# The end of the mixing in a two-block hybrid network on one core: y of the second token tile read first, x's row sums in one pass

## The reference

```python
h = rms_norm(x, g1)                 # first:  x * rsqrt(mean(x*x) + 1e-6) * g
mix = mixers(h @ w_in)              # four kinds of heads, 1024 columns
x = x + rms_norm(mix @ w_out, g2)   # y = mix @ w_out is normed by its own row sums
h = rms_norm(x, g3)
# first kind:  y = (gelu(dwconv(h @ w_gate)) * (h @ w_up)) @ w_down
# second kind: y = square(relu(h @ w_up)) @ w_down
x = x + rms_norm(y, g4)
# second kind also: x = x + sigmoid(x @ w_ple_gate) * (p @ w_ple_proj)
```

## Time and profile before

| | us |
|---|---|
| runs | 1693.14, 1697.64, 1698.69 (median 1697.64) |
| the profiled execution | 1691.87, its span 1689.8 |
| PE busy | 1594.9 (94%), granted clock 0.973 of full in the mean |
| DVE busy | 1093.3 (65%) |
| ACT busy | 776.6 (46%) |
| chain that ended last | PE 81%, DVE 10%, ACT 3% |

### The profile page before, as it was taken

One profiled execution on the slowest core, in us unless ns is written; L12 is line 12 of the kernel. 1 busy time (PEld: TensorE's weight loads), 2 busy tenths in 40 slices (PEclk: granted clock), 3 DMA queues, 4 the chain that ended last, 5 costly groups with the idle time before them and its releaser, 6 DMA issues.

```text
span 1689.8 us, 29634 instructions
## 1 busy us (share of the span) xinstructions
PE 1594.9 (94%) x12124; PEld 1425.8 (84%) x12124; DVE 1093.3 (65%) x1609; ACT 776.6 (46%) x1199; POOL 0.2 (0%) x4
## 2 busy tenths in 40 slices
PE   7998988999999989799999989999999979999998
PEld 7987568998898856799989877899889977799887
DVE  3866666776476665577754898666453798666545
ACT  4534254444435332544444455755344346655434
POOL 0000000000000000000000000000000000000000
PEclk9999898999999989899999999999999989999999
DMA  7521033555642200366554433455554432356552
GB/s 247 157 74 52 1 98 118 190 177 202 192 138 68 77 26 7 114 219 198 189 200 120 125 78 104 145 177 203 188 194 133 136 89 100 125 157 205 182 192 100
DMA packets 186310, 232.23 MB, mean 137 GB/s; under 512 B 22560, under 2 KB 161600, under 8 KB 186048
## 3 DMA queue, kind: packets, MB, share of 16 engines
q1 hardware_dynamic: 186176, 230.34, 42.2%
HBM read 229.28 MB, written 1.05 MB: 136 GB/s over the span
## 4 chain that ended last, share of the span: by engine, by line
PE 81%; DVE 10%; ACT 3%; DVEq 3%; issue 2%; DMA 1%; ACTq 0%; SPq 0%
PE banks L435 80%; DVE all_ring_rounded L2760 2%; DVE all_rest L2929 1%; DVE all_work L2864 1%; DMA all_ring<-in_w_ple_gate 1%; DVEq L2863 1%; ACT all_rest L345 1%; DVE all_work L2848 1%; DVE all_ring_rounded L1612 0%; DVE all_work L2826 0%; PE banks L930 0%; DVE all_work L2822 0%; PE banks L2242 0%; DVE x_state L384 0%; ACT all_rest L2581 0%
## 5 line engine op out<-in xcount | busy, mean ns | idle before, releaser
L435 PE MATMUL banks<-all_mix_rounded,all_ring_rounded 128*128 128x256 f32 (+2 forms) x3584 | 670.4, 288 | 20.6 <-DVEq L431 10.9
L435 PEld LDWEIGHTS banks<-all_mix_rounded,all_ring_rounded 128*128 128x128 f32 (+2 forms) x3584 | 569.6, 194 | 30.0 <-DVEq L431 11.9
L435 PE MATMUL banks<-all_work_rounded,all_ring_rounded 128*128 128x256 f32 x1792 | 512.7, 286 | 0.0
L435 PE MATMUL banks<-all_ring_rounded,all_work_rounded 128*128 128x512 f32 (+1 forms) x1856 | 461.9, 377 | 1.8 <-DVEq L2781 1.4
L435 PEld LDWEIGHTS banks<-all_ring_rounded,all_work_rounded 128*128 128x128 f32 x1856 | 347.2, 188 | 67.8 <-issue 2.7
L435 PEld LDWEIGHTS banks<-all_work_rounded,all_ring_rounded 128*128 128x128 f32 x1792 | 348.1, 194 | 1.8 <-issue 1.4
L2760 DVE TENSOR_TENSOR all_ring_rounded<-all_ring,all_ring_rounded 128x2048 fp32r<-128x2048 f32 x104 | 237.7, 2292 | 150.3 <-ACT all_ring_rounded L2577 147.6
L1612 DVE TENSOR_TENSOR all_ring_rounded<-all_ring,all_ring_rounded 128x2048 fp32r<-128x2048 f32 (+2 forms) x96 | 213.6, 2232 | 82.6 <-ACT all_ring_rounded L1369 80.5
L2577 ACT ACTIVATE all_ring_rounded<-all_ring 128x2048 fp32r<-128x2048 f32 x104 | 198.4, 1910 | 117.7 <-DMA all_ring<-in_w_mlp_down 87.3
L1369 ACT ACTIVATE all_ring_rounded<-all_ring 128x2048 fp32r<-128x2048 f32 (+2 forms) x96 | 177.7, 1858 | 112.4 <-DMA all_ring<-in_w_in 54.5
L435 PE MATMUL banks<-all_work 64*64 64x64 f32 (+10 forms) x2084 | 171.5, 271 | 18.2 <-ACTq L1544 6.0
(11 more groups left out here) (257 smaller groups left out, 1244.4 us busy)
## 6 DMA issues: line engine op xcount, KB each, us to landing
all_ring<-in_w_in SPq DMA_DIRECT2D x48, 1024.0 KB, 5.4
all_ring<-in_w_mlp_up SPq DMA_DIRECT2D x32, 1024.0 KB, 5.3
all_ring<-in_w_mlp_down SPq DMA_DIRECT2D x32, 1024.0 KB, 4.9
all_ring<-in_ffn_w_gate SPq DMA_DIRECT2D x22, 1024.0 KB, 5.3
all_ring<-in_ffn_w_up SPq DMA_DIRECT2D x22, 1024.0 KB, 5.4
all_ring<-in_ffn_w_down SPq DMA_DIRECT2D x22, 1024.0 KB, 4.9
all_ring<-in_w_out SPq DMA_DIRECT2D x16, 512.0 KB, 4.2
all_ring<-in_w_out SPq DMA_DIRECT2D x8, 1024.0 KB, 5.0
```

Of the source, the lines that this page charges most:

```text
L435: ins = self.nc.tensor.matmul(out, lhsT, rhs, start=start, stop=stop)
```

## The change

`statistics_of_x` reads both halves of a tile in one instruction of 1024 columns, writes the squares into the tile's half of `yn` and needs one small operation less. At the mixing ends ACT reads y of tile 1 before x of tile 0, with both weight panels rounded ahead of it; DVE makes both diagonals behind the addition of tile 1, and in the second kind subtracts up0 between them. In the second kind PE does one half of the product of p ahead of both transposes and the other behind them, in the two held banks of tile 1's y, and ACT copies proj0 ahead of the upper half of hT and proj1 behind its rounding.

```diff
-    def statistics_of_x(self, act, event, t, x_halves):
+    def statistics_of_x(self, act, event, t, x_halves, spare):
...
         for half in range(2):
             act.wait_ge(*x_halves[half])
-            act.drain()
-            A_(junk, self.x[:, t, 512 * half:512 * half + 512], ACT.Square, accum_out=s[:, 10 + 4 * half + t:11 + 4 * half + t])
-            if not half:
-                act.drain()
-                A_(s[:, 12 + t:13 + t], s[:, 10 + t:11 + t], ACT.Identity, bias=self.eps, scale=1.0 / DM)
         act.drain()
-        A_(s[:, 16 + t:17 + t], s[:, 14 + t:15 + t], ACT.Ln, bias=s[:, 12 + t:13 + t], scale=1.0 / DM)
+        A_(spare[:, 2 * t:2 * t + 2, :], shaped(self.x[:, t, :], 2, 512), ACT.Square, accum_out=s[:, 14 + t:15 + t])
+        act.drain()
+        A_(s[:, 16 + t:17 + t], s[:, 14 + t:15 + t], ACT.Ln, bias=self.eps, scale=1.0 / DM)
@@ ACT, first kind @@
         round_weights("gate0", "up0")
-        kit.statistics_of_x(act, 2 * layer + 1, 0, kit.x_halves(2 * layer, 0))
         kit.statistics_of_y(act, psum, 2 * layer, 1, names[1])
+        kit.statistics_of_x(act, 2 * layer + 1, 0, kit.x_halves(2 * layer, 0), yn)
+        kit.statistics_of_x(act, 2 * layer + 1, 1, kit.x_halves(2 * layer, 1), yn)
         kit.upper_half_of_hT(act, psum, "hT1", 0, PAR("pre_ffn"))
-        kit.statistics_of_x(act, 2 * layer + 1, 1, kit.x_halves(2 * layer, 1))
         kit.round_upper_half(act, 0)
@@ DVE, first kind @@
         kit.added(dve, psum, 2 * layer, 0, names[0], yn)
-        kit.scale_rows(dve, 2 * layer + 1, 0)
         subtract_rounded("gate0")
         kit.gained(dve, psum, 2 * layer, 1, names[1], gain_rows, yn)
         kit.added(dve, psum, 2 * layer, 1, names[1], yn)
+        kit.scale_rows(dve, 2 * layer + 1, 0)
+        kit.scale_rows(dve, 2 * layer + 1, 1)
         kit.lower_half_of_hT(dve, psum, "hT1", 0, PAR("pre_ffn"))
-        kit.scale_rows(dve, 2 * layer + 1, 1)
@@ PE, second kind @@
-        kit.normed_transposes(pe, psum, "hT1", norm_event(layer) + 1, 0)
         w = kit.split_panel(pe, ring, "proj")
         pe.wait_ge(*due("p_split", 1))
+        project_p(0, (None, None))
         for t in range(NT):
-            project_p(t)
+            kit.normed_transposes(pe, psum, "hT1", norm_event(layer) + 1, t)
+        project_p(1, mixed[2:4])
         kit.free_panel(ring, "proj")
-        kit.normed_transposes(pe, psum, "hT1", norm_event(layer) + 1, 1)
         psum.let_go(mixed[2:4])
@@ ACT, second kind @@
-        round_weights("proj")
-        kit.statistics_of_x(act, norm_event(layer) + 1, 0, kit.x_halves(x_event(layer), 0))
+        round_weights("proj", "up0")
         kit.statistics_of_y(act, psum, x_event_y(layer), 1, names[1])
-        round_weights("up0")
+        kit.statistics_of_x(act, norm_event(layer) + 1, 0, kit.x_halves(x_event(layer), 0), yn)
+        kit.statistics_of_x(act, norm_event(layer) + 1, 1, kit.x_halves(x_event(layer), 1), yn)
+        drain_bank("proj0", proj[:, 0, :], "proj_out")
         kit.upper_half_of_hT(act, psum, "hT1", 0, PAR("pre_mlp"))
-        kit.statistics_of_x(act, norm_event(layer) + 1, 1, kit.x_halves(x_event(layer), 1))
         kit.round_upper_half(act, 0)
         kit.upper_half_of_hT(act, psum, "hT1", 1, PAR("pre_mlp"))
         kit.round_upper_half(act, 1)
-        for i in range(2):
-            drain_bank(f"proj{i}", proj[:, i, :], "proj_out")
+        drain_bank("proj1", proj[:, 1, :], "proj_out")
@@ DVE, second kind @@
         kit.added(dve, psum, x_event_y(layer), 0, names[0], yn)
-        kit.scale_rows(dve, norm_event(layer) + 1, 0)
         subtract_rounded("proj")
         kit.gained(dve, psum, x_event_y(layer), 1, names[1], gain_rows, yn)
         kit.added(dve, psum, x_event_y(layer), 1, names[1], yn)
-        kit.lower_half_of_hT(dve, psum, "hT1", 0, PAR("pre_mlp"))
+        kit.scale_rows(dve, norm_event(layer) + 1, 0)
         subtract_rounded("up0")
         kit.scale_rows(dve, norm_event(layer) + 1, 1)
+        kit.lower_half_of_hT(dve, psum, "hT1", 0, PAR("pre_mlp"))
```

More of the change, by code:

```diff
@@ L337, in statistics_of_y @@
         A_(s[:, 8 + t:9 + t], s[:, 6 + t:7 + t], ACT.Exp, scale=-0.5).then_inc(self.sems["y_rstd"], 1)
-    def statistics_of_x(self, act, event, t, x_halves):
-        A_, s, junk = self.nc.scalar.activation, self.stat, self.junk
+    def statistics_of_x(self, act, event, t, x_halves, spare):
+        A_, s = self.nc.scalar.activation, self.stat
         for half in range(2):
             act.wait_ge(*x_halves[half])
-            act.drain()
-            A_(junk, self.x[:, t, 512 * half:512 * half + 512], ACT.Square, accum_out=s[:, 10 + 4 * half + t:11 + 4 * half + t])
-            if not half:
-                act.drain()
-                A_(s[:, 12 + t:13 + t], s[:, 10 + t:11 + t], ACT.Identity, bias=self.eps, scale=1.0 / DM)
         act.drain()
-        A_(s[:, 16 + t:17 + t], s[:, 14 + t:15 + t], ACT.Ln, bias=s[:, 12 + t:13 + t], scale=1.0 / DM)
+        A_(spare[:, 2 * t:2 * t + 2, :], shaped(self.x[:, t, :], 2, 512), ACT.Square, accum_out=s[:, 14 + t:15 + t])
+        act.drain()
+        A_(s[:, 16 + t:17 + t], s[:, 14 + t:15 + t], ACT.Ln, bias=self.eps, scale=1.0 / DM)
         act.drain()
@@ L2062, in block1 @@
     out.tensor, out.scalar, out.vector, out.load = tensor, scalar, vector, load
+    out.spare = yn
     out.transposes_in, out.upper_half_in, out.lower_half_in = transposes_in, upper_half_in, lower_half_in
@@ L2515, in tensor, with project_p @@
         p_parts = (rounded(pT), rounded(pT_lo))
-        def project_p(t):
+        def project_p(t, places):
             for half in range(2):
-                b = psum.claim(pe, f"proj{2 * t + half}")
+                b = psum.claim(pe, f"proj{2 * t + half}", places[half])
                 for cut in range(2):
@@ L3181, in _ @@
                 for t in range(NT):
-                    kit.statistics_of_x(act, 0, t, [(x_in[t], 16)] * 2)
+                    kit.statistics_of_x(act, 0, t, [(x_in[t], 16)] * 2, first.spare)
                 act.wait_ge(first.columns_in, 16)
@@ L3196, in _ @@
                         norm, add = 2 * n + 2, X_EVENT_AT_END[n]
-                        kit.statistics_of_x(act, norm, 0, kit.x_halves(add, 0))
+                        kit.statistics_of_x(act, norm, 0, kit.x_halves(add, 0), kind.spare)
                         next(ending)
@@ L3202, in _ @@
                         next(ending, None)
-                        kit.statistics_of_x(act, norm, 1, kit.x_halves(add, 1))
+                        kit.statistics_of_x(act, norm, 1, kit.x_halves(add, 1), kind.spare)
                         after.upper_half_in(act, its, 1)
```

## The result

The changed kernel took 1683.19 us in the median of 4 runs (1682.12 to 1683.52), the kernel before in the same session 1697.36 (1693.14 to 1698.69). The ratio is 0.992, 95% interval 0.9902 to 0.9938: faster by 14 us, forecast 13.0 (1684.6). Run once more on another occasion it took 1682.82 against 1694.83, ratio 0.9928, interval 0.9911 to 0.9945, so 12 us.

What follows compares the result with a forecast made beforehand. PE, busy 94%, was taken as the bound, with time to win only in its waits and low clock. First two ends 7.4, last two 5.0 and start 0.6 summed to 13.0: 1697.64 to 1684.6 us, range 1677 to 1692.

Steps and rivals of the forecast that it cites:

- The sequence at the first two ends: First and second mixing end: step times from last mix matmul to gate panel, putting both tiles' transposes in a row.
- the middle case: First two ends: tile 0's transposes at half rate, tile 1's at full; gate panel at 260.66, gain 1.75 per end.
- The full-rate case: First two ends: both tiles' transposes at full clock, gate panel at 258.93, 3.48 gained per end.
- the clock behind the start of the gate panel: First two ends: shorter low clock in the gate panel's first matmuls, gain 1.95 per end (bounds 2.75 and 0).
- Third and fourth end: Last two mixing ends: up0 starts 1.65 earlier per end, plus 1.66 of clock at the fourth; together 5.0.
- The fall at the fourth end: Fourth mixing end: the clock's drop behind PE's 2.73 wait disappears, gaining 1.66.
- The start: Start of the kernel: x's row sums in one pass bring it 0.6 earlier (bounds 0 and 0.73).
- the offset of 5.8: Whole kernel: the profiled execution lay 5.8 under the median of three runs, so the forecast started from 1697.64.
- Half rate throughout: Rival, first two ends: both tiles' transposes at half clock, no faster gate panel; 7.2 in all, 1690.4; chance 0.16.
- Swallowed: Rival, feed-forward: ends shorten, but a ring panel comes at its old time; no gain, 1697.6; chance 0.09.
- Full rate: Rival, first two ends: clock stays up in transposes and gate panel; 16.6 in all, 1681.0; chance 0.12.
- Slower: Rival, mixers: low clock moves elsewhere; three more losses like the first mixer's 6.8 make it 7.4 slower, 1705.0; chance 0.05.

Runs made afterwards that it cites:

- the short filler: Changed kernel plus 16 identity products ahead of tile 0's transposes at the first and second end: 1680.53 us, ratio 0.9917.
- the fillers: Changed kernel plus identity products at the first two ends: 32 in first wait 1686.5, 26 more in second 1685.86; 16 in first 1680.53, 13 more in second 1675.97.
- the old order: Changed kernel with the previous order on ACT, DVE and PE at the third and fourth end, one pass kept: 1689.2 us, ratio 0.9964.
- the second group: Follow-up runs sharing runs of the kernel before, whose median there was 1694.83 us; the changed kernel run again took 1682.82.
- the product between the transposes: Changed kernel with PE's previous order at the third and fourth end, p's whole product between both tiles' transposes: 1698.09 us, ratio 1.002.

## Why the prediction was right, point by point

**The sequence at the first two ends** came as worked out. Scale of y of tile 1: 1.39 behind the last mix matmul forecast, 1.43 measured. PE's idle: 4.10 and 4.09. Diagonals 1.66 apart, measured 1.73. Main path: the gate panel 13.5 behind the mix in the middle case (260.66 - 247.20), measured 13.1, 13.6, 12.9, 12.6. The full-rate case, 11.73, is what the short filler gave: 11.63. That DVE's chain is the late one there is seen in it too: PE idles 3.69 between fast transposes and the gate panel.

**The clock** behaved as the middle case said: with 4.1 us of idle ahead it fell in all four profiled ends of the changed kernel, 0.2 and 0.6 us before the transposes began in the first profile and 0.6 and 0.9 after in the second, and it came back while two tiles' transposes ran, at the second end of the first profile only 0.6 before their end: 5.34, 6.78, 5.47, 5.46, mean 5.76 against 5.83 forecast. The Trainium skill, "TensorE: Matmul & The Clock Gate", Part 1: The HAM clock gate, has the default throttled and activity releasing it; the fillers show it from both sides (3.84 with, 5.3 to 6.8 without).

**Mis-sized: the clock behind the start of the gate panel.** The sum had a gain of 1.95 per end. Before, the lower level lasted 5.6 us behind the start; after, 3.4 of it at both ends in the first profile, none and 6.0 in the second. That is about 1.2 per end (half of 5.6 less the mean 3.2), so by both profiles the term was 1.5 too large over both ends. In the first profile the stretches behind the ends got only 0.7 and 0.6 shorter where 1.95 each was forecast: 2.6 too large.

**Third and fourth end.** Forecast 12.15 (1079.5 - 1067.35), measured 11.76, since DVE's four operations take 2.63 per tile in a row, not 2.72, and the first tile began 0.2 earlier. 2.0 per end instead of 1.65. The fall at the fourth end went as forecast: 213.7 became 212.2, 1.5 against 1.66. So 5.6 instead of 5.0. With the old order it was lost again: 6 us.

**The one pass**: 1.06, as taken. In the new order it is worth 0.9 at each of the last two ends, as the passes of both tiles stand in a row behind y; the prediction had reckoned it into the steps and not told it apart.

**The start** was forecast 0.6 earlier. The transposes did start 0.70 earlier (8.36 against 9.06), but the first 64 matmuls took 8.81 instead of 7.38. The changed kernel's rows:

```profile
8.36 3.76 PE L432 MATMUL banks<-all_rest,x_state 128*128 128x128 f32 x16 [8.36 <-DVE all_rest L389]
13.49 8.81 PE L432 MATMUL banks<-all_work,all_ring 128*128 128x128 f32 x64 [1.37 <-issue]
```

and the group as the kernel before had it:

```profile
13.85 7.38 PE L435 MATMUL banks<-all_work,all_ring 128*128 128x128 f32 x64 [1.38 <-issue]
```

Over the 14 profiles of this study the group took 7.38 in eight and 8.8 to 9.5 in six, among both the kernels with one pass and those with two. The earlier start is real (8.25 to 8.82 in the eleven profiles with one pass, 9.06 to 9.21 in the three with two) and drowned by that; which of the two comes is not explained here.

**The medians.** By the first two profiles the change is worth 9.5, by the second two 14.2, by the medians 14.2 and 12.0. The first profile of before was a fast execution, 5.5 under its median; the second lies near the median, and its span is 6.0 longer, 5.0 of it by slower matmuls. The changed kernel's first profile lies 1.1 under its median. So the offset of 5.8 that the forecast carried from profile to median was right for the kernel before and too large for the changed one. The changed kernel's eight executions lie within 1.9 us of each other, the fifteen of before in the second group within 6.7; why is not shown, and it is not the number of waits alone, since the four runs with the short filler in the first wait spread over 6.5. So part of the match of 13.0 with 12 to 14 is luck. In the first profile the sum goes 13.0 - 2.6 (clock) - 1.5 (start) + 0.6 (third and fourth end) = 9.5, and a median gain 2.5 to 4.7 above that made up for it.

**The rivals.** *Half rate throughout* (7.2 in all) fell: two tiles' transposes never took 7.6. *Swallowed* fell: over two profiles of each kernel the stretches between the ends have means of 424.0, 365.5 and 381.4 after and 425.3, 365.4 and 382.0 before. *Full rate* was not the change's case but is the filler's. *Slower* fell: away from what lies just behind the ends, the recorded lower level lasts 58.0 us in both profiles of before and 58.0 and 54.6 in those of the changed kernel. It does move about, though: in the second profile of the changed kernel one such stretch in the third mixer lasted 10.2 us instead of 6.8, where others were missing. The mechanism that would have made it slower was another than the one I named, and the product between the transposes shows it: with tile 0's diagonal 3.7 later (PE idles 4.24 instead of 0.57) and nothing to do in the wait, the third and fourth end are 4 longer than before and the kernel slower.

## What to carry to other kernels

Where two tiles of a norm go through one engine's list, read the bank that is full first and fuse the small passes: but the wait then gathers in one place on the matmul engine, and it pays to fill it with independent matmuls, real ones if the stage has them (half a side product); idle ones, kept shorter than the wait, gained another 7 us here. Lay the step's latencies out as a sum from the last matmul to the next panel, for both rates of the clock; here it gave the ends to 0.4 us wherever the clock was the one assumed. Compare profiles stage by stage and medians with medians, since one execution can lie 5 us beside its median.
